# Two transformer blocks on one core: turned x copied between taps, two norms in a row at the end of the FFN, a later clear on GpSimd, and HGRN exponents ahead of the last value tile

## The reference, cut to what matters

```python
h = _rmsnorm(x, norm_ffn[layer])
u = h @ w_up                                   # 1024 -> 2 * 2816
y = conv_b + sum(u_pad[:, j:j + S, :] * conv_w[j] for j in range(3))
gate, up = jnp.split(y, 2, axis=-1)
x = x + (jax.nn.silu(gate) * up) @ w_down
```

## Time and profile before

| | us |
|---|---|
| Median of 3 runs (lowest, highest) | 1015.6 (1015.43, 1016.73) |
| The profiled execution's own time | 1011.34 |
| Its span in the profile | 1009.6 |
| Mean granted TensorE clock in it | 0.992 |

### The profile page before, as it was taken

One profiled execution on the slowest core, in us unless ns is written; L12 is line 12 of the kernel. 1 busy time (PEld: TensorE's weight loads), 2 busy tenths in 40 slices (PEclk: granted clock), 3 DMA queues, 4 the chain that ended last, 5 costly groups with the idle time before them and its releaser, 6 DMA issues. The chain is left out here.

```text
span 1009.6 us, 19673 instructions
## 1 busy us (share of the span) xinstructions
PE 978.9 (97%) x7864; PEld 919.4 (91%) x7864; DVE 763.7 (76%) x1296; ACT 552.1 (55%) x873; POOL 66.8 (7%) x54
## 2 busy tenths in 40 slices
PE   7999999999999999999999999999999998999998
PEld 5999999898788999899999999999997898999996
DVE  5765776867887768498667888788868667788886
ACT  4644555365666656553566555555675464555552
POOL 3100004000000410000030000000001420000000
PEclk9999999999999999999999999999999998999999
DMA  9644445793212556500464767575531454766661
GB/s 279 178 128 131 130 146 154 219 298 110 84 43 83 156 180 187 190 1 1 148 187 134 210 198 208 167 212 164 153 125 43 125 153 139 206 180 200 192 184 42
DMA packets 184434, 153.16 MB, mean 152 GB/s; under 512 B 12509, under 2 KB 176932, under 8 KB 184356
## 3 DMA queue, kind: packets, MB, share of 16 engines
q1 hardware_dynamic: 184146, 152.01, 51.1%
q10 hardware_dynamic: 210, 0.05, 0.0%
HBM read 148.91 MB, written 1.05 MB: 149 GB/s over the span
## 5 line engine op out<-in xcount | busy, mean ns | idle before, releaser
L447 PE MATMUL bank<-h_high,w_high 128*128 128x256 f32 x1312 | 372.2, 284 | 4.8 <-DVE work L2013 1.5
L448 PE MATMUL bank<-h_low,w_high 128*128 128x256 f32 x1312 | 364.9, 278 | 0.0
L449 PE MATMUL bank<-h_high,w_low 128*128 128x256 f32 x1312 | 364.7, 278 | 0.0
L399 ACT ACTIVATE w_high<-ring 128x2048 fp32r<-128x2048 f32 x137 | 261.8, 1914 | 138.7 <-PE bank L449 131.4
L409 DVE TENSOR_TENSOR w_low<-ring,w_high 128x2048 fp32r<-128x2048 f32 x118 | 270.3, 2292 | 25.7 <-ACT w_high L399 25.2
L447 PEld LDWEIGHTS bank<-h_high,w_high 128*128 128x128 f32 x1312 | 248.2, 189 | 7.1 <-issue 5.4
L448 PEld LDWEIGHTS bank<-h_low,w_high 128*128 128x128 f32 x1312 | 248.3, 189 | 0.8 <-issue 0.5
L449 PEld LDWEIGHTS bank<-h_high,w_low 128*128 128x128 f32 x1312 | 248.1, 189 | 0.0
L1116 ACT ACTIVATE ffn_conv<-ffn_normed,par 128x256 f32<-128x256 f32 x88 | 48.1, 594 | 68.0 <-DVE ffn_normed L1129 67.9
L1138 DVE SCALAR_TENSOR_TENSOR ffn_conv<-ffn_normed,par,ffn_conv 128x254 f32<-128x254 f32 (+1 forms) x176 | 77.1, 480 | 7.4 <-ACT ffn_conv L1116 2.3
L795 ACT ACTIVATE work<-bank,work 128x128 f32<-128x128 f32 (+1 forms) x112 | 47.7, 432 | 47.5 <-DVE work L777 36.7
(11 more groups left out here) (359 smaller groups left out, 1873.4 us busy)
## 6 DMA issues: line engine op xcount, KB each, us to landing
ring<-in_ffn_w_up_dram SPq DMA_DIRECT2D x44, 1024.0 KB, 6.1
ring<-in_ffn_w_down_dram SPq DMA_DIRECT2D x22, 1024.0 KB, 5.2
ring<-in_fox_w_in_dram SPq DMA_DIRECT2D x16, 1024.0 KB, 6.0
ring<-in_hgrn_w_in_dram SPq DMA_DIRECT2D x16, 1024.0 KB, 5.5
ring<-in_nsa_w_in_dram SPq DMA_DIRECT2D x14, 1024.0 KB, 5.8
ring<-in_fox_w_out_dram SPq DMA_DIRECT2D x4, 1024.0 KB, 5.1
ring<-in_nsa_w_out_dram SPq DMA_DIRECT2D x4, 1024.0 KB, 5.2
ring<-in_hgrn_w_out_dram SPq DMA_DIRECT2D x4, 1024.0 KB, 5.4
```

The lines of the kernel that those rows point to most:

```text
L399: i = nc.scalar.activation(dst, src, ACT.Copy)
L447: nc.tensor.matmul(o, ah, bh, start=start, stop=False, **kw)
L448: nc.tensor.matmul(o, ah, bl, start=False, stop=False, **kw)
L449: return nc.tensor.matmul(o, al, bh, start=False, stop=stop, **kw)
```

## The change

It has four parts. (1) In the feed-forward layer, the second `turn_x` quarter stays behind pair 1 and the first goes into its middle; ACT copies quarter 0 ahead of the tap of pair 0, quarter 1 behind it, quarters 2 and 3 behind the gate of pair 1. A dummy Silu stands ahead of the first tap. DVE norms pair 1 before it multiplies pair 0. (2) For the last two pairs, 20 and 21, DVE norms both before it convolves either, and ACT does both taps before both gates. (3) GpSimd's clear of `kz2` waits for `n_row` of NSA's norm. (4) In HGRN, PE sums half 1 of head 0 ahead of the last value tile, ACT takes its Exp in place of the dummy one, half 1 of a later head waits for one Exp fewer, and the spread of the norm stands two chunks later in tile t_f + 1. (1) applies to both layers except for what concerns `turn_x`; (2) to both.

```diff
--- before.py
+++ after.py
...
-def ffn_pair(pe, t, u, bank_wait, ready=None, later=0, quarter=None):
+def ffn_pair(pe, t, u, bank_wait, ready=None, later=0, quarter=None, half=None):
...
                 quarter()
+            if half and (e, c) == (0, DC - 1):
+                half()
     mm.then_inc(tile_done, 1)
...
+        def copy_rows(act, q):
+            act.wait_ge(x_in_rows, q + 1)
+            nc.scalar.activation(x_rows[:, q // 2, q % 2 * 512:(q % 2 + 1) * 512], B[3 - q % 2][:, :],
+                                 ACT.Copy).then_inc(x_copied, 1)
+
         def rows_program(pe):
-            ffn_pair(pe, pair_tile(1), u0 + 1, (u0 + 1) // 2, quarter=lambda: nrm.spread(pe))
-            turn_x(pe, 0)
+            ffn_pair(pe, pair_tile(1), u0 + 1, (u0 + 1) // 2, quarter=lambda: nrm.spread(pe),
+                     half=lambda: turn_x(pe, 0))
             turn_x(pe, 1)
...
             high(act, t0 + 3)
+            nc.scalar.activation(scratch[:, :], eps[:, :], ACT.Silu)
+            if not following:
+                copy_rows(act, 0)
             for j in range(2):
                 tap(act, j)
+                if not following and j == 0:
+                    copy_rows(act, 1)
                 high(act, t0 + 4 + j)
...
             if not following:
-                for q in range(4):
-                    act.wait_ge(x_in_rows, q + 1)
-                    nc.scalar.activation(x_rows[:, q // 2, q % 2 * 512:(q % 2 + 1) * 512], B[3 - q % 2][:, :],
-                                         ACT.Copy).then_inc(x_copied, 1)
+                copy_rows(act, 2)
+                copy_rows(act, 3)
...
                     two_pairs(2 + 2 * g, 6 + 3 * g, i)
-            for g in range(2):
-                two_pairs(18 + 2 * g, 30 + 3 * g)
+            two_pairs(18, 30)
+            for j in (20, 21):
+                tap(act, j)
+            for j in (20, 21):
+                gate(act, j)
             next_high(act, t0 + NTILE)
...
-            one_pair(0, 3)
-            one_pair(1, 4)
+            normed(dve, 0)
+            low(dve, nc.vector, t0 + 3)
+            convolve(dve, 0)
+            normed(dve, 1)
+            multiply(dve, 0)
+            low(dve, nc.vector, t0 + 4)
+            convolve(dve, 1)
+            multiply(dve, 1)
             with dve.Fori(0, NLOOP) as i:
...
                     two_pairs(2 + 2 * g, 5 + 3 * g, i)
-            for g in range(2):
-                two_pairs(18 + 2 * g, 29 + 3 * g)
+            two_pairs(18, 29)
+            normed(dve, 20)
+            normed(dve, 21)
+            low(dve, nc.vector, t0 + 32)
+            for j in (20, 21):
+                convolve(dve, j)
+                multiply(dve, j)
             low(dve, nc.vector, t0 + NTILE)
...
         nc.gpsimd.memset(xb.rearrange("p i (n k) -> p i n k", n=2)[:, :, :, NG:HD], 0.0).then_inc(nsa_cleared, 1)
+        pool.wait_ge(n_row, nrm_nsa.n + 1)
         for b in range(2):
...
         for i in range(1, 4):
-            by_feature(pe, t_f + i, hsp, between=lambda q, i=i: (i, q) == (1, 0) and nrm_hgrn.spread(pe))
+            by_feature(pe, t_f + i, hsp, ready=lambda c, i=i: (i, c) == (1, 6) and nrm_hgrn.spread(pe))
         for i in range(4):
...
             mm.then_inc(lf_turned, 1)
-        for i in range(4):
-            by_token(pe, t_i + i, hsp)
-        pe.wait_ge(lf_split, 4)
-        pe.wait_ge(levels_in, 1)
-
-        def exponents(w):
-            hh, tt = w // 2, w % 2
-            if w == 0:
+        def exponents(hh, tt):
+            n = 2 * hh + 1 - tt
+            if n == 1:
                 evacuated(pe, t_i + 2)
                 evacuated(pe, t_i + 3)
-            if w >= 2:
-                pe.wait_ge(decayed, max(2, w - 1))
+            if n >= 2:
+                pe.wait_ge(decayed, n - 1)
             for b in range(2):
...
             mm.then_inc(summed, 1)
+
+        for i in range(4):
+            if i == 3:
+                pe.wait_ge(lf_split, 4)
+                pe.wait_ge(levels_in, 1)
+                exponents(0, 1)
+            by_token(pe, t_i + i, hsp)
...
             if k < HG_H:
-                exponents(2 * k + (k == 0))
-                exponents(2 * k + (k > 0))
+                if k:
+                    exponents(k, 1)
+                exponents(k, 0)
             if 1 <= k <= HG_H:
...
             nc.scalar.activation(a[:, 2 * i:2 * i + 2, :], a[:, 2 * i:2 * i + 2, :], ACT.Silu).then_inc(done, 1)
+
+        def exps(hh, tt):
+            n = 2 * hh + 1 - tt
+            act.wait_ge(summed, n + 1)
+            if hh >= 2:
+                act.wait_ge(scored, 2 * hh - 2)
+            for b in range(2):
+                i = nc.scalar.activation(dec[:, hh % 2, 4 * b:4 * b + 4, tt * P:(tt + 1) * P],
+                                         B[2 * tt + b][:, :].rearrange("p (l t) -> p l t", l=4), ACT.Exp)
+            i.then_inc(decayed, 1)
...
             if i == 3:
-                nc.scalar.activation(scratch[:, :], eps[:, :], ACT.Exp)
+                exps(0, 1)
             act.wait_ge(tile_done, t_i + i + 1)
...
-        def exps(w):
-            hh, tt = w // 2, w % 2
-            act.wait_ge(summed, w + 1 if hh else 2 - w)
-            if hh >= 2:
-                act.wait_ge(scored, 2 * hh - 2)
-            for b in range(2):
-                i = nc.scalar.activation(dec[:, hh % 2, 4 * b:4 * b + 4, tt * P:(tt + 1) * P],
-                                         B[2 * tt + b][:, :].rearrange("p (l t) -> p l t", l=4), ACT.Exp)
-            i.then_inc(decayed, 1)
-
         for k in range(HG_H + 3):
             if k < HG_H:
-                exps(2 * k + (k == 0))
-                exps(2 * k + (k > 0))
+                if k:
+                    exps(k, 1)
+                exps(k, 0)
             if k == 1:
```

## The result

| | before | after |
|---|---|---|
| Median (lowest, highest) of the first comparison, 4 runs each, us | 1015.62 (1015.43, 1016.73) | 1000.17 (998.74, 1001.31) |
| The profiled execution's own time, us | 1011.34 | 999.53 |
| Its span, us | 1009.6 | 997.8 |
| Mean granted clock in it | 0.992 | 0.997 |

The ratio is 0.9843, 95% interval 0.9828 to 0.9859: 15.4 us less. Yet the two profiled executions lie 11.81 us apart, and the sum of the steps was 11.6.

A forecast was written before the change was run, and what follows sets the result against it. PE, busy 97% of the span, was taken as the bound, with only its waits and low clock to win. Terms 7.0 + 0.8 + 1.8 + 1.7 + 0.7 - 0.4 = 11.6 us off the 1015.6 median gave 1004.0, range 1001.8 to 1007.2.

The forecast's parts named there:

- Second layer: start: Second feed-forward layer's start: earlier copies of turned x end PE's 4.1 us wait and the half clock behind it, 7.0 us less.
- Second layer: end: End of the second feed-forward layer: PE's wait for the last hidden chunk goes, 1.7 us less.
- First layer: start and end: First feed-forward layer: PE's waits before pair 3 (0.8 us) and for the last hidden chunk (1.8 us) both go.
- NSA: NSA's start: with the clears later, two short DVE instructions run quicker and PE's wait goes, 0.7 us less.
- HGRN from the first value tile to the feed-forward layer: HGRN: moving half 1's sums ahead delays DVE's mix of head 0, 0.4 us more (0.1 less to 0.9 more).
- Clears hold DVE: NSA rival: a clear blocks DVE's low, PE waits 2.0 us more and the 0.7 is lost, 1006.7 us; chance 0.06.
- The clock falls in HGRN: HGRN rival: PE's short waits, now close together, bring half clock costing 2.0 us, 1006.0 us; chance 0.10.
- A low-clock stretch elsewhere better: Rival: the later MLA stretch stays at full clock, winning half of some 3.5 us, or HGRN is better, 1002.3 us; chance 0.09.
- DVE falls behind: Second feed-forward layer's loop rival: without the 4 us wait DVE loses its lead, up to 1016.8 us; chance 0.05.
- The dummy Silu: Feed-forward start rival: it leaves the 1.28 us table load in pair 0's gate, first layer loses 0.6, 1004.6 us; chance 0.03.

The follow-up runs named there:

- before_c: The kernel before, unchanged, run again in the fourth session: 1011.85 us (12 runs), ratio 0.999.
- before_again: The kernel before, unchanged, run again in the first session: 1014.27 us (12 runs), ratio 1.0012.
- b_norm1: The kernel before, with DVE norming pair 1 ahead of multiply 0 in the first feed-forward layer alone: 1012.21 us (12 runs), ratio 1.0007.
- after_again: The changed kernel, unedited, run once more for the spread of its runs: 1001.42 us (11 runs), ratio 0.9928.
- after_c: The changed kernel, unedited, run in the fourth session beside the kernel before: 999.05 us (6 runs), ratio 0.9874.
- u_hgrn_c: The changed kernel with HGRN's head 0 sums behind the last value tile again, new order of halves kept, fourth session: 1000.04 us (6 runs), ratio 0.9904.
- u_hgrn_again: The changed kernel with HGRN's half 1 sums and Exp behind the last value tile, repeated in the third session: 1000.88 us (6 runs), ratio 0.9894.
- u_hgrn: The changed kernel with HGRN's sums and Exp of half 1 behind the last value tile again, first session: 999.43 us (6 runs), ratio 0.9883.
- b_relax: The kernel before, with half 1 first in every HGRN head and one Exp fewer to wait for: 1009.58 us (12 runs), ratio 0.9974.

## Why the prediction was wrong, and where it was right

**The steps, by the two profiled executions.**

| Step | forecast, us | trace, us |
|---|---|---|
| Second layer: start | -7.0 | -6.75 |
| Second layer: end | -1.7 | -1.76 |
| First layer: start and end | -0.8 - 1.8 | -2.74 |
| NSA | -0.7 | -0.72 |
| HGRN from the first value tile to the feed-forward layer | +0.4 (-0.1 to +0.9) | +0.76 |
| Stretch 357 to 399 (behind half clock, 117.8 to 364 where before had 113.3: 0.15; two matmuls late at 364.5: 0.2, cause not shown) | 0 | +0.36 |
| MLA stretch at 767 to 771 at full clock (-0.82), pitch from there to the second layer (-0.13) | 0 | -0.95 |
| Sum | -11.6 | -11.8 |

The copies, the norm order, the two norms in a row and the clears did what the steps said, with every wait gone that should go. HGRN was costed at 0.4: to the sums of head 7 it is 0.47, right; another 0.2 is the wait before the output tile (0.69 for 0.50), which I hadn't followed. The steps add up to their sum, but that the total agrees to 0.2 us is also luck: two things that nobody planned (+0.36 and -0.95) and HGRN's excess (0.36) nearly cancel.

**The step that failed** is the last of the working: "The median of the runs is 1015.6, 4.3 more than that execution, which these rows don't explain; I take the same 11.6 from it". The difference of 4.3 us was taken as a constant that both kernels carry. No run shows such a constant. What the runs show is a pitch that changes from execution to execution and makes one layer 5.7 us longer. Profiled executions have it so:

| Profiled execution | time, us | pitch in the first / second layer |
|---|---|---|
| before | 1011.34 | 113.3 / 113.3 |
| before_c | 1011.03 | 113.3 / 113.3 |
| before_again | 1014.88 | 117.8 / 113.3 |
| b_norm1 (wait moved, not gone) | 1015.60 | 117.8 / 113.3 |
| after, after_again, after_c | 999.53, 1000.14, 999.46 | 113.3 / 113.3 |
| u_hgrn_c | 996.7 | 113.3 / 113.3 |
| u_hgrn_again | 1003.01 | 117.8 / 113.3 |
| u_hgrn | 1004.64 | 113.3 / 117.8 |

(In after_again, u_hgrn and u_hgrn_c the last 8 us of the first layer's loop are at 117.8, which is 0.3 us.)

The kernel before ran 116 more times in the later sessions: median 1011.6, between 1006.64 and 1019.72, and 27 of these runs, fewer than one in four, lie above 1015.4, where all four of the first comparison lay. With those four its 120 runs have a median of 1011.7 and a mean of 1012.6; 21 runs of the changed kernel have 1000.1 and 1001.2. The distance is 11.6 us in the median and 11.4 in the mean, and the profiles give 11.8. So the gain of the change is what the steps said, and what the first comparison has above it, 3.8 us of its 15.4, lies in which runs it happened to hold. That the four runs of before had a slow layer each is inferred from their time; no profile of them exists. It was an unusual set: if runs are independent, four in a row above 1015.4 have a chance of 0.3% (27/116 to the fourth power), so something of that session can't be ruled out.

That the runs of before fall into two groups shows when those of the same mean granted clock are put side by side (the three clocks with the most runs, 89 of the 116):

| Granted clock | lower runs, us | upper runs, us |
|---|---|---|
| 0.992 | 15 at 1010.43 to 1012.09 | 4 at 1016.74 to 1017.46 |
| 0.993 | 22 at 1008.24 to 1011.61 | 20 at 1014.44 to 1016.95, 3 at 1018.44 to 1019.72 |
| 0.995 | 14 at 1006.89 to 1009.88 | 11 at 1013.17 to 1016.13 |

At each clock there is a gap of about 3 to 5 us that no run fills. The profiled execution with a slow layer lies above it (1014.88 at 0.995), the two with none below (1011.34 and 1011.03 at 0.992). Without the sorting the clock, worth some 3 us between 0.992 and 0.995, hides the gap. 38 of these 89 runs are upper ones; the three highest fit two slow layers, which no profile shows.

**The rivals.** *Clears hold DVE* fell for the `low`, which took 2.28 us beside the clears. The Trainium skill (GPSIMD Engine Reference, Specifications) lists contention with VectorE instructions that have two SBUF inputs, or run in a 2-port perf mode. For the first kind the trace doesn't agree where the other side is a memset: the `low` has two SBUF inputs. What a clear did hold is the small half of the inverse root, as the forecast read it from the earlier trace rows; whether that one runs in a 2-port mode no run here shows. *The clock falls in HGRN* fell: no stretch of HGRN's heads is under 1 in the profile after, with waits of 1.02, 0.26 and 0.69 us; the rule that the prediction put beside it doesn't show in HGRN. *A low-clock stretch elsewhere better* came true by itself in the profile after (MLA, 0.82 us), while other executions have such a stretch at 786 or 793: its place is not the kernel's. *DVE falls behind* fell: 841.33 to 977.80 after, 851.37 to 987.84 before, 136.47 us both. *The dummy Silu* took the load off the gate (821.01).

**What stays open.** What makes the pitch one or the other isn't known. Behind the waits of 3.9 us and more in the feed-forward layers, which went through half clock, it was 113.3 each time; behind half clock near 357, short gaps and single transposes it was either. Whether the change also makes the slow pitch rarer, by taking out the wait before pair 3, isn't settled: 5 of 21 runs of the changed kernel lie about 5 us above the rest, and 38 of 89 of before, which may be chance; `b_relax` kept the wait and had none of 12; and profiles with a slow first layer exist on both sides. No version was found that beats the changed kernel beyond the spread.

## What to carry to other kernels

Work the steps out on one profiled execution, and when its time and the median of the runs disagree, don't carry the difference over as a constant: look for something that the profile can show (here, the number of matmuls in windows of equal length at full clock), sort the runs by their granted clock, and ask for more runs of the kernel before, since its median moves the forecast as much as the change does. Removing a wait is only worth its row if nothing arrives late right behind it; a stop of 0.09 us was left in `b_norm1`, and the slow pitch began at it. A change of several parts hides its losing part: undoing them one at a time found 0.93 us in HGRN that the total never showed.

## What was unexpected of the hardware

At a granted clock of 1.00, with PE busy throughout, 256-column matmuls ran at 113.3 or at 117.8 ns from start to start, each for stretches of 160 us and more; a feed-forward layer costs 5.7 us more at the second. One transpose in the stream could change it, at four of eight places in one execution. And a DVE instruction of 0.17 us on 128 x 2 stood until one of POOL's two clears had ended, in four executions the second (3.21 us), in three the first (1.3 us), while a DVE instruction of 2.28 us with two SBUF inputs beside the same clears lost nothing.
